# The first input weights asked for ahead of the fourth prompt tile in a decoder layer's projection

## The reference

```python
def _rmsnorm(x, g):
    y = xf * lax.rsqrt(jnp.mean(xf * xf, axis=-1, keepdims=True) + RMS_EPS) * g
def _project(h, lp, pos):
    z = h @ lp['w_in']
    q, kc, vc, ks, vs, kw, vw, g_nsa, u, g_mrg = jnp.split(z, _split_points(), axis=-1)
def _ssm(u, h0, lp):
    step = jnp.exp(lp['ssm_log_dt'])[:, None]
    a_bar = jnp.exp(lam * step)                     # lam = a_re + i a_im
    b_bar = ((a_bar - 1.0) / lam)[..., None] * (b_re + i b_im)
    bu = jnp.einsum('gpc,btgc->btgp', b_bar, uf)
    # scan h[t] = a_bar * h[t-1] + bu[t];  y = Re(c h) + d u
```

## Time and profile before

| | |
|---|---|
| time, median of 3 runs | 1943.53 us (1942.11 to 1944.89) |
| the profiled execution's own time | 1943.15 us |
| its span | 1941.5 us |
| TensorE matmul busy | 1493.8 us (77%) |
| VectorE busy | 1183.8 us (61%) |
| POOL busy | 640.8 us (33%) |
| ScalarE busy | 340.7 us (18%) |
| mean granted TensorE clock | 0.784 of full speed |

### The profile page before, as it was taken

One profiled execution on the slowest core, in us unless ns is written; L12 is line 12 of the kernel. 1 busy time (PEld: TensorE's weight loads), 2 busy tenths in 40 slices (PEclk: granted clock), 3 DMA queues, 4 the chain that ended last, 5 costly groups with the idle time before them and its releaser, 6 DMA issues.

```text
span 1941.5 us, 22167 instructions
## 1 busy us (share of the span) xinstructions
PE 1493.8 (77%) x7427; PEld 663.7 (34%) x7427; DVE 1183.8 (61%) x2950; ACT 340.7 (18%) x846; POOL 640.8 (33%) x747
## 2 busy tenths in 40 slices
PE   6999999999878889867777666656566666665676
PEld 5568765477734555412343211100001111110111
DVE  7590363236668786455778974478985455444445
ACT  5562354202322221011111010010000000000001
POOL 3602143004722333323333343333333333333332
PEclk9999999999988998977888766565665655566655
DMA  6336524556899999999999999999999999999997
GB/s 203 117 112 176 194 85 171 216 195 199 306 419 418 407 417 402 413 418 413 398 409 399 405 409 413 414 421 413 397 409 417 419 412 417 416 415 412 413 420 287
DMA packets 141477, 669.61 MB, mean 345 GB/s; under 512 B 17268, under 2 KB 50228, under 8 KB 71412
## 3 DMA queue, kind: packets, MB, share of 16 engines
q0 software_dynamic: 75648, 546.87, 68.9%
q1 hardware_dynamic: 65716, 121.33, 18.0%
HBM read 661.00 MB, written 19.65 MB: 351 GB/s over the span
## 4 chain that ended last, share of the span: by engine, by line
DMA 34%; PE 24%; DVE 9%; issue 7%; POOL 4%; ACT 1%; DVEq 0%; POOLq 0%
DMA uv<-in_peer_uv,idxT 22%; DMA w_out<-in_peer_uv,idxT 12%; PE ex_acc L2608 10%; PE ex_hb L2502 4%; PE ro_pq L2073 3%; POOL uv L2393 2%; DVE uv L2776 2%; POOL w_out L2393 1%; PE ro_ps L2049 1%; DVE w_out L2776 1%; PE ex_late L2527 1%; PE ex_late L2575 1%; PE ex_pick L2555 1%; PE ex_late L2542 1%; DVE ch_iu L1832 1%
## 5 line engine op out<-in xcount | busy, mean ns | idle before, releaser
L2502 PE MATMUL ex_hb<-ffn_gain,spread 24*128 24x512 bf16 x1040 | 348.9, 495 | 398.0 <-DVE uv L2776 263.5
L2776 DVE SCALAR_TENSOR_TENSOR uv<-uv,ex_hb 128x1024 f32<-128x1024 f32 x344 | 416.3, 1219 | 316.3 <-DMA uv<-in_peer_uv,idxT 278.2
L2393 POOL DMA_INDIRECT uv<-in_peer_uv,idxT x340 | 321.0, 944 | 598.6 <-PE ex_acc L2608 520.6
L2776 DVE SCALAR_TENSOR_TENSOR w_out<-w_out,ex_hb 128x1024 f32<-128x1024 f32 x176 | 213.3, 1219 | 153.1 <-DMA w_out<-in_peer_uv,idxT 124.9
L2502 PEld LDWEIGHTS ex_hb<-ffn_gain,spread 24*128 24x128 bf16 x1040 | 54.0, 99 | 732.0 <-DVE uv L2776 398.2
L2608 PE MATMUL ex_acc<-uv,wts 128*32 128x512 f32 x1376 | 275.7, 944 | 0.0
L2393 POOL DMA_INDIRECT w_out<-in_peer_uv,idxT x172 | 162.4, 944 | 307.9 <-PE ex_acc L2608 266.6
L2927 ACT ACTIVATE ex_gelu<-ex_dots 128x4 f32<-128x4 f32 (+1 forms) x131 | 26.9, 205 | 952.6 <-DVE uv L2776 647.8
L2608 PE MATMUL ex_acc<-w_out,wts 128*32 128x512 f32 x704 | 145.4, 961 | 0.0
L2608 PEld LDWEIGHTS ex_acc<-uv,wts 128*32 128x32 f32 x1376 | 47.4, 146 | 158.8 <-issue 158.8
L2575 PE MATMUL ex_late<-hx,sgT 128*128 128x264 f32 x256 | 66.7, 418 | 0.0
(11 more groups left out here) (552 smaller groups left out, 2042.8 us busy)
## 6 DMA issues: line engine op xcount, KB each, us to landing
sgT<-in_late_w SPq DMA_DIRECT2D x24, 1024.0 KB, 9.4
uv<-in_peer_w_q SPq DMA_DIRECT2D x15, 1024.0 KB, 8.0
gate_ring<-in_w_in SPq DMA_DIRECT2D x6, 2048.0 KB, 9.4
uv<-in_peer_uv,idxT POOLq DMA_INDIRECT x344, 13.7
ks_rows<-in_ks_pages SPq DMA_DIRECT2D x64, 64.0 KB, 2.1
vs_rows<-in_cache_v_sel SPq DMA_DIRECT2D x64, 64.0 KB, 2.1
gate_ring<-in_kc_pages SPq DMA_DIRECT2D x64, 64.0 KB, 2.1
de_ks<-ks_rows SPq DMA_DIRECT2D x8, 512.0 KB, 9.5
```

Source lines behind the costliest of these rows:

```text
L2393: pool.indirect_dma_start(slot(s).rearrange("p j n -> p (j n)"), None, table, bass.IndirectOffsetOnAxis(ap=S.idxT[:, t:t + 1], axis=0))\
L2502: last = pe.matmul(hb[s % 2][:, CHUNK * h:CHUNK * h + CHUNK], spread[p, k % LOAD, :], h_rows[p, l % 2, CHUNK * h:CHUNK * h + CHUNK], start ...
L2776: dve.scalar_tensor_tensor(out=rows_, in0=rows_, scalar=1.0, in1=hb[s % 2][:], op0=ALU.mult, op1=ALU.mult, accum_out=dots[:, B % 2, c:c + ...
```

## The change

The request for chunk 0 of the input weights is issued behind the request of the third prompt tile (t == 2), ahead of the fourth, of the samples and of the rates. The request itself, its place in SBUF and its semaphore are the same. The other chunks keep their places; the loop's own request is left out for chunk 0.

```diff
+            def load_columns(c):
+                c0, n, what = chunks[c]
+                src = w_heads if c == 1 else w_in[:, :, c0:c0 + n]
+                sp.dma_start(ring[:, c % 2, :, 0:n], src).then_inc(w_landed[c % 2], 16)
+
             for t in range(4):
                 sp.dma_start(x[t], io["x_prompt"][0, P * t:P * t + P, :]).then_inc(xt_landed[t], 16)
                 if t == 1:
                     sp.dma_start(gain[:], io["norm_mix"][0, :].partition_broadcast(P)).then_inc(E["gain_in"], 16)
+                if t == 2:
+                    load_columns(0)
             sp.wait_ge(E["pads_zero"], 1)
             sp.dma_start(last_x[0:NB, :], io["x_sample"].rearrange("b a n -> (b a) n")).then_inc(xt_landed[4], 16)
...
-            for c, (c0, n, _w) in enumerate(chunks):
+            for c in range(len(chunks)):
                 if c >= 2:
                     sp.wait_ge(E["z_done"], ends[c - 2])
-                src = w_heads if c == 1 else w_in[:, :, c0:c0 + n]
-                sp.dma_start(ring[:, c % 2, :, 0:n], src).then_inc(w_landed[c % 2], 16)
+                if c:
+                    load_columns(c)
```

## The result

| | before | changed |
|---|---|---|
| median, same chip | 1943.31 us (22 runs) | 1946.45 us (22 runs) |
| spread | 1940.15 to 1948.32 | 1944.86 to 1949.90 |
| ratio | | 1.0016 (95% interval 1.0009 to 1.0022) |
| projection over | 172.5 us | 175.2 us |

The change makes the kernel slower by 0.16%, 3.1 us; the interval is 1.7 to 4.3 us. What can be compared to a tenth of a microsecond is where the first stages end.

A forecast was written before the change was run, and what follows sets the result against it. TensorE was taken to bound the kernel to 427 us; its 2.6 us earlier start is lost waiting for VectorE's chain, 2.5 us late, so 1943.15 plus 2.5, with 0.38 to the median, gives 1946.0 us, range 1941.0 to 1949.0.

The forecast's parts named there:

- the likeliest case: Whole kernel: the fourth tile lands late and delays VectorE's chain, +2.1 to +3.1 us, chance 0.63.
- VectorE's chain: Projection, scale of tiles 3 and 4 to copies of u: starts at 19.3 instead of 16.84, fourth group at 47.6.
- TensorE-bound to 427 us, so a shift comes through: Whole kernel: no slack to speak of on TensorE up to 427 us, so a projection shift reaches the end nearly in full.
- The fourth tile: Projection's start: lands at 17.1 instead of 11.7, so ScalarE squares it 2.5 us after today's 14.63.
- The weights: Projection's start: first weights land at 15.7 instead of 18.25; TensorE's first projecting matmul starts 2.6 us earlier.
- lower end: Weights' landing from below: third tile's arrival at 9.96 plus 5.4 us on the wire, 15.35.
- upper end: Weights' landing from above: today's 18.25 less 1.35 for the fourth tile and 0.55 for the rates, 16.35.
- Six requests leave SP 0.6 us later: SP's queue: requests of fourth tile, samples, a_im, a_re and two of log_dt each leave 0.6 us later, costing nothing.
- The early start by itself: Rival, projection: TensorE starts 2.6 us earlier and everything follows, 1940.9 us; chance 0.07.
- overtake the weights: Rival, DMA queue: the fourth tile lands by 14.6, before ScalarE needs it, no change, 1943.5 us; chance 0.11.
- held back to 18.5 or more: Rival, DMA queue: the fourth tile lands much later, at 19.4, chain 4.8 us late, 1948.3 us; chance 0.19.

The follow-up runs named there:

- e3: Against before: the fourth tile's request put last, behind the first weights, which stay behind the rates; ratio 1.0023, projection over at 177.5 us.
- e8: The changed kernel with 12 useless matmuls in TensorE's wait ahead of the fourth group; ratio to before 1.0031, projection over at 177.3 us.
- e6: Before's requests, ScalarE squaring tiles 3 and 4 ahead of its last two copies of turned tiles; ratio to before 0.9992, projection over at 171.2 us.
- e10: Before's requests, exponents and sines ahead of squares and norms of tiles 3 and 4, three useless matmuls; run twice, ratio to before 0.9991 both times.
- e1: Against before: first weights asked for behind the fourth tile and samples, ahead of the rates; whole not timed, projection over at 172.1 us.
- e2: Against before: first weights asked for behind the fourth tile, ahead of samples and rates; whole not timed, projection over at 173.8 us.
- e7: Against before: the edits of e1 and e6 together; ratio 0.9998, projection over at 171.5 us.
- e4: The changed kernel with rates asked for right ahead of the weights, exponents and sines ahead of the fourth tile's work; ratio to before 0.9992.
- e8b: The changed kernel with 6 useless matmuls in TensorE's wait ahead of the fourth group; ratio to before 1.0021, projection over at 175.3 us.
- e9: e7 with 17 useless matmuls, 12 ahead of the first transposes and 5 behind the first four; ratio to before 1.0016, projection over at 176.4 us.

## Why the prediction was right

The time, 1946.45 against 1946.0 forecast, lies in the range, and the likeliest case is the one that came. That it came within 0.5 us is partly luck: a loss of 2.5 us was forecast, the measured one of 3.1 is known to 1.7 to 4.3, and before's median was 0.2 us lower than the one I added to. The stage's end shows 2.7 us, of which 2.4 are VectorE's chain (the fourth group at 47.53 in place of 45.17) and the rest the clock, which the sum didn't have. Point by point:

- *TensorE-bound to 427 us, so a shift comes through.* Right: 2.7 us at 173, 3.0 at 427, 3.1 at the end. Over the timed experiments the whole follows the stage's end within its intervals: e3 (+5.0 us) came out at +0.23%, 2.3 to 6.6 us; e8 (+4.8) at 3.9 to 8.4.
- *The fourth tile.* Forecast to land at 17.1 and to be squared 2.5 us late; it landed at 17.0 and was squared 2.39 us late. Two errors cancel in this: the weights landed 0.5 us sooner than forecast, and the tile 1.8 us behind them, where I had 1.4. e3, which delays nothing but this tile, makes the loss by itself.
- *VectorE's chain.* Start forecast at 19.3, was 19.24; wait 6.3, was 6.5; the stretch from there to the end of the copies took 28.1 us, 28.2 before; fourth group forecast at 47.6, was 47.53. The best evidence that no slack is hidden in this chain is the column "plus": 26.57 to 26.62 us in eight kernels, over exponents from 17.5 to 21.8.
- *The weights.* Forecast 15.7, landed 15.2, just under my lower end of 15.35. The lower end was the third tile's arrival (9.96) plus 5.4 us, and 15.7 was that and 0.4. In the profile after, the third tile's square started at 9.65, and the weights landed 0.15 us past that plus 5.4. The upper end of 16.35 was further off, by its term for the rates: 0.55 us, worked out from bytes not moved in 10.5 to 12.5. With the rates ahead of the weights TensorE started at 17.55 to 18.43 (before, e6, both e10), with them behind at 16.84 to 16.90 (e1, e2, e7); with the fourth tile behind too it was 16.59 and 17.63 (e3, e4) against 15.28 to 15.91 (changed, e8, e8b). So the rates cost between 0.65 and 2.35 us by these pairs. The pairs differ by other things as well: where the same requests stand ahead of it, the third tile was squared anywhere from 9.22 to 10.27, and whether the small packets cost this or the later issue of the weights behind them isn't separated. It did no harm here, as TensorE's start isn't on the path. The Trainium skill, DMA: Bandwidth & Descriptors, Rules for kernel authors, says that transfers under 64 KB are mostly overhead; these four together hold 24 KB, 0.06 us at 391 GB/s, and the runs agree.
- *Six requests leave SP 0.6 us later.* Off: log_dt leaves 2.6 us later, skip 1.6, as single issues behind the weights took up to 1.41 us. The second weights' request at 14.75 is even 0.5 us earlier than before. It cost nothing, as forecast.
- *What was missed.* That the wait isn't only idle time: the granted clock falls to 0.50 in it and the group behind is 1.4 us longer. A wait of 1.0 us for VectorE ahead of the strips, in before

```profile
53.51 1.92 PE L758 MATMUL pz<-gate_ring,hx 128*32 128x512 f32 x16 [0.99 <-DVE uT L261]
```

  took up most of it; 0.2 to 0.3 us came through. Without that cover it would have been 1.4. The Trainium skill, TensorE: Matmul & The Clock Gate, Part 1, calls the throttled state the default, which activity releases; the rows of the changed kernel and of e8b, at 0.50 and at 1.00 behind the same wait without and with work in it, agree.
- *The rivals.* The early start by itself brought nothing in e1 and e7. The queue didn't let the tile overtake the weights: it landed 1.8 us behind them. Nor was it held back to 18.5 or more.

## What to carry to other kernels

A load asked for earlier moves every load behind it, and each of those has a first user of its own. Write down for each the time it lands and the time it is first wanted: here the weights had a wait of 4.3 us in view, but the fourth tile had 2.9 us of slack for a transfer of 5.4. Follow the engine that waits to the next place where it waits: the longest wait in the list (4.3 us, DMA) was worth nothing, as a second, of 1.1 us for VectorE, stood behind it. And where a group always starts a fixed time after some small instruction (26.6 us after the exponent), that instruction is the one to move; e6 and e10, which leave all loads alone and change only the engines' orders (e10 has three filling matmuls besides), ended the stage earlier than any place for the request did.

## What the runs showed of the hardware

- After waits of about 6.3 us TensorE's granted clock was at 0.50. It came back between 49.5 and 51.5 in the changed kernel (2 to 4 us into the group) and only past 53.5 in e3 (over 5 us in), so the same wait cost 1.4 us of the group in one execution and 2.8 in the other.
- A wait of over 2 us can be enough, and need not be: behind 2.25 us (e2) and 2.42 us (e9) the clock was still at 1.00 when the group started, fell to 0.50 within about 1 us and stayed there for some 3 us, and the group took 9.04 us; behind 2.39 us (e1) it stayed at 1.00 and the group took 7.36. The length of the wait alone doesn't decide.
- In before the first group took 5.56 us for 16 matmuls where later ones took 3.62, at a granted clock shown as 1.00. Work right ahead of it (e9, e10) brought 3.62 and 3.69. In four traces it is the slow clock: e1, e3, e6 and e8b show 0.50 in this group (5.38, 5.35, 6.66 and 5.38 us). Before, changed, e2, e4, e7 and e8 show 1.00 for groups as long (5.48 to 6.61 us); that the clock was at 0.50 in these too, unrecorded, is inferred from their times and not shown. The first row is e3's, the second the changed kernel's:

```profile
18.40:19.40 1.00, 1.00 (x4) 0.50 1.08 394
```

```profile
18.40:19.40 1.00, 1.00 (x4) 1.00 1.09 408
```

- 24 KB of rates in small packets ahead of 2 MB went with a start of TensorE 0.65 to 2.35 us later, over the pairs of executions named above.
